# The low half of a weight split by an accumulating SBUF-to-SBUF DMA, in a two-layer float32 encoder

## Chip, cores and metric

One NeuronCore of a Trainium2 chip runs the whole program. The metric is the device time of one execution in microseconds, the median of the runs; smaller is better.

## The reference, cut to what matters

```
for l in range(2):
    hn = rms_norm(h, mix_norm_g[l])
    h = h + (diff_hgrn_mixer(hn, ...) if l == 0 else short_conv_mixer(hn, ...))
    hn = rms_norm(h, mlp_norm_g[l])
    h = h + jnp.square(jax.nn.relu(hn @ mlp_w_up[l])) @ mlp_w_down[l]
return rms_norm(h, final_norm_g)
```

x is 256 x 2048 in float32. Layer 0's mixer has one input projection of 2048 x 8192 (eight heads of differential attention with ALiBi and eight of a two-way gated recurrence) and an output projection of 2048 x 2048. Layer 1's mixer is `(b_gate * conv3(c_gate * h)) @ w_out`, with an input projection of 2048 x 6144 and an output of 2048 x 2048. Each MLP has 2048 x 8192 up and 8192 x 2048 down. All is float32, and the weights, 400 MB in all, are read once.

## The kernel before

**The split of a weight.** TensorE multiplies in float32r. To keep float32's accuracy, every operand is held as a high part (rounded to float32r) and a low part (the rest), and each product is three matmuls: high by high, high by low, low by high. The activations are split once (xT_hi, xT_lo, yT_hi, yT_lo), the weights as they stream in.

**Slots and halves.** The weights come in 400 slots of 1 MB (128 rows x 4 x 512 float32), numbered through the program: 64 for layer 0's input (PROJ_AT), 16 for its output (OUT_AT), 128 for the first MLP (MLP0_AT), 64 for the convolution layer (CONV_AT), 128 for the second MLP (MLP1_AT). `raw` holds RAW = 4 slots. A slot is split in two halves (k = 0 and 1) of 128 x 1024, and w_hi and w_lo are rings of HALVES = 4 halves. So halves 2s and 2s + 1 belong to slot s and half j takes the place of half j - 4.

The engines take a slot in this order:

- SyncE, `load` (L295 to L305): waits until the low parts of slot s - 4 are done, and issues the DMA of slot s into `raw`. From the first MLP on it is one DMA of 1 MB, before that four of 256 KB.
- ScalarE, `split_hi` (L314 to L327): waits for the landing and, for each half, until the half four before has been used by TensorE (`w_used`); then the activation of L326 copies `raw` to w_hi, rounding.
- VectorE, `split_lo` (L329 to L339): waits for `hi_ready`; L337 is w_lo = raw - w_hi, and counts `lo_ready` up by one.
- TensorE, `multiply` (L341 to L359, 12 matmuls of 512 columns a half) or `multiply_T` (L361 to L381, 24 of 256 columns): waits for `lo_ready` of its half and counts `w_used` up at its end.

ScalarE and VectorE stand two slots ahead: while TensorE is at slot s, they split slot s + 2. All queues are in order and written out by hand, one program for each engine; loops (`Fori`) cover the repeated blocks.

**The stages that the change touches.** An MLP (`mlp` in each engine's program) has 16 blocks of 512 hidden columns, each with four up slots (`multiply_T`, result with the hidden units on partitions) and four down slots (`multiply`). In the block's course ScalarE makes the ReLU and the square of the up product (L1072, L1077) and its high part (L1087), VectorE its low part (L1419) and the sums into h (L1195). The convolution layer has 48 input slots in `multiply_T` form and 16 output slots.

**GpSimd (POOL).** Its program is busy in layer 0 (`mix`). After that it only does `rstd_of(n)` for the four later norms (L516, L519, L520), each behind VectorE's sum of squares, and, between norm 2 and norm 3, four products cg = cg * rows2 (L638), each behind VectorE's product of L1459. It issues no DMA.

**The end.** SyncE loads the final norm's gains into raw slot 0 (L474) when slot TOTAL - 4 is split; VectorE scales h by them (L1560), and SyncE stores.

Of the kernel before, what the change touches and what calls it, by code (L numbers as in the profile page):

```python
# [27 lines left out]
F32 = mybir.dt.float32  # L28
F32R = mybir.dt.float32r
U32 = mybir.dt.uint32  # L30
ALU = mybir.AluOpType
ACT = mybir.ActivationFunctionType
AX_X = mybir.AxisListType.X

P = 128
T = 256
# [3 lines left out]
CB = D // 512  # L40
# [5 lines left out]
RAW = 4  # L46
HALVES = 4
# [5 lines left out]
FF_BLOCKS = FF // 512  # L53
MLP_SLOTS = FF_BLOCKS * 8
MLP0_AT = OUT_AT + 16
CONV_AT = MLP0_AT + MLP_SLOTS
CONV_SLOTS = CB * 16
MLP1_AT = CONV_AT + CONV_SLOTS
TOTAL = MLP1_AT + MLP_SLOTS
# [39 lines left out]
def build(nc, x, mix_norm_g, mlp_norm_g, final_norm_g, ab_w_in, ab_w_out, diff_lambda, diff_subln_g,  # L99
          hgrn_lb, hgrn_norm_g, conv_w_in, conv_w, conv_w_out, mlp_w_up, mlp_w_down, out):  # L100
    with ExitStack() as ctx:
        def sb(name, shape, dt=F32):
            return ctx.enter_context(nc.sbuf_tensor(name, shape, dt))
# [4 lines left out]
        def sem(name):  # L108
            return ctx.enter_context(nc.semaphore(name))


        raw = sb("raw", [P, RAW, 4, 512])
        w_hi = sb("w_hi", [P, HALVES, 2, 512], F32R)
        w_lo = sb("w_lo", [P, HALVES, 2, 512], F32R)
# [54 lines left out]
        cg = proj_a[:, :, :, :].rearrange("p a b c -> p (a b c)").rearrange(  # L169
            "p (a b) -> p a b", b=T)  # L170
        cT = lq[:, 1]
        rows2 = bias[:, 0]
# [11 lines left out]

        landed = [sem(f"landed{i}") for i in range(RAW)]
        hi_ready = sem("hi_ready")
        lo_ready = sem("lo_ready")
        w_used = sem("w_used")
        x_in = [sem(f"x_in{i}") for i in range(CB)]
# [6 lines left out]
        pair_read = [sem(f"pair_read{i}") for i in range(2)]  # L196
# [14 lines left out]
        u_ready = sem("u_ready")  # L211
# [38 lines left out]
        def h_read(n):  # L250

            return PAIR_MLP0 + 1 if isinstance(n, int) and n == 0 else n * 3 + (PAIR_MLP0 - 1)
# [29 lines left out]
        def count(scale, const, base, step, i):  # L282

            if isinstance(i, int):
                return scale * (base + step * i) + const
            return i * (scale * step) + (scale * base + const)

        def stand_alone(eng, n):


            if not isinstance(n, int):
                eng.sem_inc(waited, 1)


        def load(sp, base, step, i, src, pieces=1):  # L295

            slot = base % RAW
            if base >= RAW:

                sp.wait_ge(lo_ready, count(2, 2 - 2 * RAW, base, step, i))  # L300
            if pieces == 1:
                sp.dma_start(raw[:, slot], src).then_inc(landed[slot], 16)
                return
            for q in range(pieces):
                sp.dma_start(raw[:, slot, q], src(q)).then_inc(landed[slot], 16)  # L305

        def landed_at(base, step, i):


            each, before = (64, 0) if base < MLP0_AT else (16, 48 * (MLP0_AT // RAW))  # L310
            uses = base // RAW + 1
            return i * (each * step // RAW) + (each * uses + before)

        def split_hi(eng, base, step, i, ks=(0, 1)):  # L314
            if base >= TOTAL:
                return
            slot = base % RAW
            if 0 in ks:

                eng.wait_ge(landed[slot], landed_at(base, step, i))  # L320
            for k in ks:
                ring = (2 * base + k) % HALVES
                if 2 * base + k >= HALVES:

                    eng.wait_ge(w_used, count(2, k + 1 - HALVES, base, step, i))
                nc.scalar.activation(w_hi[:, ring], raw[:, slot, 2 * k:2 * k + 2], ACT.Copy  # L326
                                     ).then_inc(hi_ready, 1)  # L327

        def split_lo(eng, base, step, i, ks=(0, 1)):  # L329
            if base >= TOTAL:  # L330
                return
            slot = base % RAW
            for k in ks:
                ring = (2 * base + k) % HALVES

                eng.wait_ge(hi_ready, count(2, k + 1, base, step, i))
                nc.vector.tensor_tensor(w_lo[:, ring], raw[:, slot, 2 * k:2 * k + 2],  # L337
                                        w_hi[:, ring].bitcast(F32), ALU.subtract
                                        ).then_inc(lo_ready, 1)  # L339

        def multiply(eng, base, step, i, hi, lo, kt0, dst, first, last, ks=(0, 1)):  # L341

            for k in ks:
                ring = (2 * base + k) % HALVES

                eng.wait_ge(lo_ready, count(2, k + 1, base, step, i))
                for q in range(2):
                    kt = kt0 + 2 * k + q
                    begin = first and k == ks[0] and q == 0
                    end = last and k == ks[-1] and q == 1  # L350
                    for tt in range(NT):
                        cols = slice(tt * P, (tt + 1) * P)
                        nc.tensor.matmul(dst[:, tt], hi[:, kt, cols], w_hi[:, ring, q],  # L353
                                         start=begin, stop=False)
                        nc.tensor.matmul(dst[:, tt], hi[:, kt, cols], w_lo[:, ring, q],  # L355
                                         start=False, stop=False)
                        mm = nc.tensor.matmul(dst[:, tt], lo[:, kt, cols], w_hi[:, ring, q],  # L357
                                              start=False, stop=end)
                mm.then_inc(w_used, 1)  # L359

        def multiply_T(eng, base, step, i, kt0, dst, first, last):  # L361

            for k in range(2):
                ring = (2 * base + k) % HALVES

                eng.wait_ge(lo_ready, count(2, k + 1, base, step, i))
                for q in range(2):
                    kt = kt0 + 2 * k + q
                    end = last and k == 1 and q == 1
                    for c in range(4):  # L370
                        cols = slice(c * P, (c + 1) * P)


                        begin = first and k == 0 and q == 0 and c % 2 == 0
                        nc.tensor.matmul(dst[:, c], w_hi[:, ring, q, cols], xT_hi[:, kt],  # L375
                                         start=begin, stop=False)
                        nc.tensor.matmul(dst[:, c], w_hi[:, ring, q, cols], xT_lo[:, kt],  # L377
                                         start=False, stop=False)
                        mm = nc.tensor.matmul(dst[:, c], w_lo[:, ring, q, cols], xT_hi[:, kt],  # L379
                                              start=False, stop=end and c % 2 == 1)  # L380
                mm.then_inc(w_used, 1)  # L381
# [9 lines left out]
        def _(sp):  # L391
# [25 lines left out]
            with sp.Fori(0, HEADS - 1) as i:  # L417
                for p in range(8):
                    load(sp, 8 + p, 8, i,
                         lambda q: head_columns(p // 4, p % 4, bass.ds(i + 1, 1))(q)  # L420
                         .rearrange("p a b n -> p (a b) n"), 4)
# [48 lines left out]
            mlp(MLP1_AT, 1)  # L470


            sp.wait_ge(lo_ready, 2 * (TOTAL - 4) + 2)
            sp.dma_start(raw[:, 0], final_norm_g.rearrange("(a c n) -> a c n", a=1, n=512)  # L474
                         .broadcast_to([P, 4, 512])).then_inc(fin_rows, 16)
            for cb in range(CB):
# [9 lines left out]
        def _(pool):  # L486
# [4 lines left out]
                                    base=0, pattern=[[-1, P]], channel_multiplier=1  # L491
# [21 lines left out]
            def rstd_of(n):  # L513

                pool.wait_ge(sq_sum, n + 1)
                nc.gpsimd.tensor_scalar(meansq[:], meansq[:], 1.0 / D, EPS, ALU.mult, ALU.add  # L516
                                        ).then_inc(rstd_step, 1)
                pool.wait_ge(rstd_step, 2 * n + 1)
                nc.gpsimd.tensor_tensor(rstd[:, n], meansq[:], minus_half[:, 0:NT], ALU.pow)  # L519
                nc.gpsimd.tensor_tensor(rstd2[:, n], meansq[:], minus_one[:], ALU.pow  # L520
                                        ).then_inc(rstd_step, 1)

            rstd_of(0)
            for d in range(2):
                for lv in range(7):
# [5 lines left out]
                                            base=-lo, pattern=[[-2 * m, 64 // m], [0, m]],  # L531
# [4 lines left out]
                                            base=lo + m - 1, pattern=[[2 * m, 64 // m], [0, m]],  # L536
# [91 lines left out]
            with pool.Fori(0, HEADS - 1) as i:  # L628
                mix(i)
            mix(HEADS - 1)  # L630
            for n in range(1, 5):
                rstd_of(n)
                if n == 2:

                    pool.wait_ge(r2_row, 1)
                    for b in range(CB):
                        pool.wait_ge(pair_read[1], h_read(b))
                        nc.gpsimd.tensor_tensor(cg, cg, rows2.unsqueeze(1).broadcast_to([P, 4, T]),  # L638
                                                ALU.mult).then_inc(u_ready, 1)


        def gain_transpose_pe(n, cb):

# [942 lines left out]
```

## Time and profile before

| what | value |
| --- | --- |
| median of 3 runs | 2364.97 us (2364.95 to 2365.18) |
| the profiled execution: its span, first to last instruction | 2362.9 us |
| own time of the profiled execution beside its span | not listed apart; the median stands 2.1 us over the span |
| TensorE matmuls busy | 2332.4 us, 99% |
| VectorE busy | 1462.6 us, 62% |
| ScalarE busy | 1090.2 us, 46% |
| GpSimd busy | 249.8 us, 11% |
| load queue's packets, share of 16 DMA engines | 56.4% |

The span is cut by stage: layer 0's mixer up to about 530 us, the first MLP to about 1240, the convolution layer to about 1610, the second MLP to 2350, and the end. "Busy" is the time in which an engine runs an instruction; waits and the issue of DMAs don't count. Matmuls are pipelined: one of 512 columns shows 389 ns, but the next starts before it ends.

### The profile page before, as it was taken

How to read it: one execution, taken by the hardware profiler on the slowest of the kernel's cores; microseconds unless marked ns; L12 is line 12 of the kernel's file. 1: busy time of each engine (PE TensorE's matmuls, PEld its weight loads, DVE VectorE, ACT ScalarE, POOL GpSimd, SP SyncE). 2: the span in 40 equal slices, each digit the busy share in tenths (PEclk: the TensorE clock that was granted, in tenths of full speed). 3: DMA queues.
4: the chain of work that ended last, by engine and by line, in shares of the span. 5: the costliest groups of instructions: out<-in, count | busy, mean ns of one | idle time of the engine just before them, and what ended most of it. 6: DMA issues, size and time to landing. Idle time of an engine off the chain costs nothing.

```text
span 2362.9 us, 38313 instructions
## 1 busy us (share of the span) xinstructions
PE 2332.4 (99%) x14581; PEld 2108.1 (89%) x14581; DVE 1462.6 (62%) x1686; ACT 1090.2 (46%) x1391; POOL 249.8 (11%) x367
## 2 busy tenths in 40 slices
PE   8999999999999999999999999999999999999997
PEld 6888888789899999999989999998998998998996
DVE  5777777755565565565566564656555556555655
ACT  5555554435444444444445334345444444444443
POOL 4445555500000000000000000000000000000000
PEclk9999999999999999999999999999999999999999
DMA  9555555455555555555555555555555555555553
GB/s 257 162 154 157 145 152 166 145 177 170 189 192 181 192 182 194 180 193 182 190 188 176 187 180 183 192 179 178 194 180 194 181 193 182 191 183 189 189 184 125
DMA packets 316175, 425.78 MB, mean 180 GB/s; under 512 B 10537, under 2 KB 141906, under 8 KB 315986
## 3 DMA queue, kind: packets, MB, share of 16 engines
q1 hardware_dynamic: 316066, 424.92, 56.4%
q8 instruction: 43, 0.70, 0.1%
q14 instruction: 18, 0.15, 0.0%
q10 hardware_dynamic: 48, 0.02, 0.0%
HBM read 422.79 MB, written 2.10 MB: 180 GB/s over the span
## 4 chain that ended last, share of the span: by engine, by line
PE 87%; POOL 6%; issue 4%; ACT 1%; DVE 1%; SPq 1%; DMA 0%; POOLq 0%; DVEq 0%; ACTq 0%
PE pair L353 14%; PE pair L355 14%; PE pair L357 14%; PE m L379 11%; PE m L377 11%; PE m L375 11%; PE pair L379 3%; PE pair L375 3%; PE pair L377 3%; POOL lk L577 1%; PE m L726 1%; POOL even L564 1%; POOL kin L577 1%; PE m L790 1%; POOL lk L589 1%
## 5 line engine op out<-in xcount | busy, mean ns | idle before, releaser
L337 DVE TENSOR_TENSOR w_lo<-raw,w_hi 128x1024 fp32r<-128x1024 f32 x800 | 988.8, 1242 | 855.5 <-ACT w_hi L326 854.5
L326 ACT ACTIVATE w_hi<-raw 128x1024 fp32r<-128x1024 f32 x800 | 846.2, 1059 | 1219.3 <-PE pair L357 633.6
L379 PE MATMUL m<-xT_hi,w_lo 128*128 128x256 f32 x2176 | 615.8, 283 | 0.0
L377 PE MATMUL m<-xT_lo,w_hi 128*128 128x256 f32 x2176 | 615.8, 283 | 0.0
L375 PE MATMUL m<-xT_hi,w_hi 128*128 128x256 f32 x2176 | 615.6, 283 | 0.0
L353 PE MATMUL pair<-w_hi,yT_hi 128*128 128x512 f32 x1280 | 499.8, 391 | 1.0 <-DVE h L1208 0.9
L355 PE MATMUL pair<-w_lo,yT_hi 128*128 128x512 f32 x1280 | 498.4, 389 | 0.0
L357 PE MATMUL pair<-w_hi,yT_lo 128*128 128x512 f32 x1280 | 498.1, 389 | 0.0
L375 PEld LDWEIGHTS m<-xT_hi,w_hi 128*128 128x128 f32 x2176 | 417.7, 192 | 1.2
L377 PEld LDWEIGHTS m<-xT_lo,w_hi 128*128 128x128 f32 x2176 | 417.7, 192 | 1.2
L379 PEld LDWEIGHTS m<-xT_hi,w_lo 128*128 128x128 f32 x2176 | 417.7, 192 | 0.0
L353 PEld LDWEIGHTS pair<-w_hi,yT_hi 128*128 128x128 f32 x1280 | 240.4, 188 | 50.8 <-DVE h L1208 1.4
L357 PEld LDWEIGHTS pair<-w_hi,yT_lo 128*128 128x128 f32 x1280 | 240.3, 188 | 50.3
L355 PEld LDWEIGHTS pair<-w_lo,yT_hi 128*128 128x128 f32 x1280 | 240.5, 188 | 48.1
L1195 DVE SCALAR_TENSOR_TENSOR h<-pair,rstd,h 128x512 f32<-128x512 f32 x288 | 202.0, 743 | 5.8 <-PE pair L357 5.8
L353 PE MATMUL pair<-w_hi,xT_hi 128*128 128x512 f32 x512 | 204.1, 399 | 0.0
L357 PE MATMUL pair<-w_hi,xT_lo 128*128 128x512 f32 x512 | 200.0, 391 | 0.0
L355 PE MATMUL pair<-w_lo,xT_hi 128*128 128x512 f32 x512 | 199.7, 390 | 0.0
L375 PE MATMUL pair<-xT_hi,w_hi 128*128 128x256 f32 x640 | 181.6, 284 | 0.0
L379 PE MATMUL pair<-xT_hi,w_lo 128*128 128x256 f32 x640 | 181.1, 283 | 0.0
L377 PE MATMUL pair<-xT_lo,w_hi 128*128 128x256 f32 x640 | 181.1, 283 | 0.0
L516 POOL TENSOR_SCALAR meansq<-meansq 128x2 f32<-128x2 f32 x5 | 1.0, 193 | 1607.4 <-DVE meansq L1188 1607.4
(147 smaller groups left out, 1711.0 us busy)
## 6 DMA issues: line engine op xcount, KB each, us to landing
raw<-in_mlp_w_up SPq DMA_DIRECT2D x128, 1024.0 KB, 5.2
raw<-in_mlp_w_down SPq DMA_DIRECT2D x128, 1024.0 KB, 5.0
raw<-in_ab_w_in SPq DMA_DIRECT2D x256, 256.0 KB, 3.9
raw<-in_conv_w_in SPq DMA_DIRECT2D x48, 1024.0 KB, 5.2
raw<-in_ab_w_out SPq DMA_DIRECT2D x64, 256.0 KB, 4.1
raw<-in_conv_w_out SPq DMA_DIRECT2D x16, 1024.0 KB, 5.0
h<-in_x SPq DMA_DIRECT2D x4, 512.0 KB, 5.9
out_dram<-h SPq DMA_DIRECT2D x8, 256.0 KB, 2.4
```

The lines of the kernel that those rows point to most:

```text
L326: nc.scalar.activation(w_hi[:, ring], raw[:, slot, 2 * k:2 * k + 2], ACT.Copy).then_inc(hi_ready, 1)
L337: nc.vector.tensor_tensor(w_lo[:, ring], raw[:, slot, 2 * k:2 * k + 2], w_hi[:, ring].bitcast(F32), ALU.subtract).then_inc(lo_ready, 1)
L353: nc.tensor.matmul(dst[:, tt], hi[:, kt, cols], w_hi[:, ring, q], start=begin, stop=False)
L355: nc.tensor.matmul(dst[:, tt], hi[:, kt, cols], w_lo[:, ring, q], start=False, stop=False)
L357: mm = nc.tensor.matmul(dst[:, tt], lo[:, kt, cols], w_hi[:, ring, q], start=False, stop=end)
L375: nc.tensor.matmul(dst[:, c], w_hi[:, ring, q, cols], xT_hi[:, kt], start=begin, stop=False)
L377: nc.tensor.matmul(dst[:, c], w_hi[:, ring, q, cols], xT_lo[:, kt], start=False, stop=False)
L379: mm = nc.tensor.matmul(dst[:, c], w_lo[:, ring, q, cols], xT_hi[:, kt], start=False, stop=end and c % 2 == 1)
L564: nc.gpsimd.tensor_tensor(both(even, lv)[:, :, :, 1], first[:, :, 0::2], second[:, :, 0::2], ALU.mult)
L577: mark(nc.gpsimd.tensor_tensor(dst.rearrange("p (a b) -> p a b", b=m), src.rearrange("p (a b) -> p a b", b=m), factor.unsqueeze(2).broadca ...
L589: mark(nc.gpsimd.tensor_copy(dst.rearrange("p (a b c) -> p a b c", b=2, c=m)[:, :, 1], kin[:, 1].rearrange("p (a b c) -> p a b c", b=2, c= ...
L1195: ins = nc.vector.scalar_tensor_tensor(out=h[:, tt, cols], in0=pair[cb % 2][:, tt], scalar=factor[:, tt:tt + 1], in1=h[:, tt, cols], op0=A ...
```

## The change

From slot MLP0_AT on, the second half (k = 1) of each of the 320 slots gets its low part in another way. ScalarE writes, behind the high part of that half, w_lo = -raw, rounded to float32r as the high part is (an activation with a scale of -1.0, counted by `neg_ready`). GpSimd waits for it and issues a DMA within SBUF that adds raw to w_lo, 128 rows x 1024 float32, 512 KB (`add_lo`, `accum_op=ALU.add`, counted by `lo_added`, one semaphore for each raw slot, 16 for each DMA). The sum is raw minus its rounded value, the same low part. VectorE's subtraction for that half goes; the first halves (k = 0) and all of layer 0's mixer stay as they are.

TensorE waits for `lo_added` in front of second halves (`wait_lo`), and SyncE's `load` for both `lo_added` and `lo_ready` of the slot that it overwrites. GpSimd's program gets the 320 DMAs in slot order, with `rstd_of` and the four products of the convolution layer placed between them (`mlp_los`, `scale_u`).

```diff
             slot = base % RAW
+            if base >= MLP0_AT + RAW:
+                sp.wait_ge(lo_added[slot], lo_added_at(base - RAW, step, i))
+                stand_alone(sp, i if step else 0)
             if base >= RAW:
-                sp.wait_ge(lo_ready, count(2, 2 - 2 * RAW, base, step, i))
+                sp.wait_ge(lo_ready, lo_at(base - RAW, step, i, 1))
...
+        def wait_lo(eng, base, step, i, k):
+            if base >= MLP0_AT and k == 1:
+                eng.wait_ge(lo_added[base % RAW], lo_added_at(base, step, i))
+            else:
+                eng.wait_ge(lo_ready, lo_at(base, step, i, k))
...
                 nc.scalar.activation(w_hi[:, ring], raw[:, slot, 2 * k:2 * k + 2], ACT.Copy
                                      ).then_inc(hi_ready, 1)
+                if base >= MLP0_AT and k == 1:
+                    nc.scalar.activation(w_lo[:, ring], raw[:, slot, 2:4], ACT.Copy, scale=-1.0
+                                         ).then_inc(neg_ready, 1)
+
+        def add_lo(pool, base, step, i):
+            slot, ring = base % RAW, (2 * base + 1) % HALVES
+            pool.wait_ge(neg_ready, count(1, 1 - MLP0_AT, base, step, i))
+            stand_alone(pool, i if step else 0)
+            pool.dma_start(w_lo[:, ring].bitcast(F32), raw[:, slot, 2:4], accum_op=ALU.add
+                           ).then_inc(lo_added[slot], 16)
...
             for k in ks:
+                if base >= MLP0_AT and k == 1:
+                    continue
...
-                eng.wait_ge(lo_ready, count(2, k + 1, base, step, i))
+                wait_lo(eng, base, step, i, k)
...
-            sp.wait_ge(lo_ready, 2 * (TOTAL - 4) + 2)
+            sp.wait_ge(lo_ready, lo_at(TOTAL - 4, 0, 0, 0))
+            sp.wait_ge(lo_added[0], lo_added_at(TOTAL - 4, 0, 0))
...
+            def mlp_los(at, n):
+                for p in range(4):
+                    add_lo(pool, at + p, 0, 0)
                 rstd_of(n)
+                for p in range(4):
+                    add_lo(pool, at + 4 + p, 0, 0)
+                with pool.Fori(0, FF_BLOCKS - 1) as i:
+                    for p in range(8):
+                        add_lo(pool, at + 8 + p, 8, i)
...
+            mlp_los(MLP0_AT, 1)
+            for p in range(12):
+                if p == 4:
+                    rstd_of(2)
+                if p == 10:
                     pool.wait_ge(r2_row, 1)
+                    scale_u(0)
+                add_lo(pool, CONV_AT + p, 0, 0)
+            with pool.Fori(0, CB - 2) as i:
+                for p in range(16):
+                    if p == 10:
+                        scale_u(i + 1)
+                    add_lo(pool, CONV_AT + 12 + p, 16, i)
...
+            mlp_los(MLP1_AT, 3)
+            rstd_of(4)
```

## Rows read from the trace of the kernel before

**Rows 1.** The page: busy time of each engine over the span
```profile
span 2362.9 us, 38313 instructions
PE 2332.4 (99%) x14581; PEld 2108.1 (89%) x14581; DVE 1462.6 (62%) x1686; ACT 1090.2 (46%) x1391; POOL 249.8 (11%) x367
```

**Rows 2.** Busy time in stretches: one up, one down product, the changed stages, the end
```profile
core 0: us, PE busy (x) PEld busy (x) DVE busy (x) ACT busy (x) POOL busy (x), PEclk, DMA share, GB/s
702.50:725.50 23.00, 23.00 (x194) 23.00 (x193) 12.32 (x12) 9.51 (x10) 0.00 (x0) 1.00 0.57 184
725.50:747.30 21.80, 21.80 (x99) 18.04 (x98) 13.76 (x14) 10.39 (x12) 0.00 (x0) 1.00 0.59 189
537.00:2350.00 1813.00, 1813.00 (x12018) 1676.08 (x12016) 1065.63 (x1100) 815.38 (x944) 14.26 (x13) 1.00 0.56 184
2350.00:2362.90 12.90, 0.06 (x1) 0.00 (x0) 6.96 (x11) 1.45 (x4) 1.55 (x3) 0.70 0.45 163
```

**Rows 3.** ScalarE's timeline in one MLP block: start, length, what, idle before
```profile
705.42 1.06 ACT L326 ACTIVATE w_hi<-raw 128x1024 fp32r<-128x1024 f32 x1 [1.81 <-PE m L379]
708.30 1.06 ACT L326 ACTIVATE w_hi<-raw 128x1024 fp32r<-128x1024 f32 x1 [1.82 <-PE m L379]
...
725.58 1.06 ACT L326 ACTIVATE w_hi<-raw 128x1024 fp32r<-128x1024 f32 x1 [1.82 <-PE m L379]
726.55 1.06 ACT L1072 ACTIVATE sm<-m 128x512 f32<-128x512 f32 x2
727.50 1.15 ACT L1077 ACTIVATE sm<-sm 128x512 f32<-128x512 f32 x2
728.54 1.06 ACT L326 ACTIVATE w_hi<-raw 128x1024 fp32r<-128x1024 f32 x1
731.04 1.06 ACT L326 ACTIVATE w_hi<-raw 128x1024 fp32r<-128x1024 f32 x1 [1.45 <-PE pair L357]
733.76 1.06 ACT L326 ACTIVATE w_hi<-raw 128x1024 fp32r<-128x1024 f32 x1 [1.66 <-PE pair L357]
736.48 1.06 ACT L326 ACTIVATE w_hi<-raw 128x1024 fp32r<-128x1024 f32 x1 [1.66 <-PE pair L357]
```

**Rows 4.** Groups of instructions, one MLP block (702.5 to 747.3)
```profile
L337 DVE TENSOR_TENSOR w_lo<-raw,w_hi 128x1024 fp32r<-128x1024 f32 x16 | 19.6, 1225 | 18.7 <-ACT w_hi L326 18.7
L326 ACT ACTIVATE w_hi<-raw 128x1024 fp32r<-128x1024 f32 x16 | 17.0, 1060 | 24.9 <-PE m L379 13.5 <-PE pair L357 11.4
```

**Rows 5.** One load: issue; DMA in 40 slices from 738.9 to 744.9; one full us
```profile
738.97 0.37 SPq L302 DMA_DIRECT2D raw<-in_mlp_w_up  x1
...
DMA  0000000377799989888999999999973000000000
q1 hardware_dynamic: 528, 1.05, 53.0%
raw<-in_mlp_w_up SPq DMA_DIRECT2D x1, 1024.0 KB, 5.1
...
742.00:743.00 1.00, 1.00 (x6) 0.84 (x5) 0.00 (x0) 0.98 (x1) 0.00 (x0) 1.00 1.04 406
```

**Rows 6.** GpSimd's timeline from 530 on: start, length, what, idle before
```profile
564.79 0.19 POOL L516 TENSOR_SCALAR meansq<-meansq 128x2 f32<-128x2 f32 x1 [79.94 <-DVE meansq L1188]
565.07 0.70 POOL L519 TENSOR_TENSOR rstd<-meansq,minus_half 128x2 f32<-128x2 f32 x1
565.74 0.70 POOL L520 TENSOR_TENSOR rstd<-meansq,minus_one 128x2 f32<-128x2 f32 x1
...
1315.56 2.40 POOL L638 TENSOR_TENSOR proj_a<-proj_a,bias 128x1024 f32<-128x1024 f32 x1 [28.49 <-DVE proj_a L1459]
```

**Rows 7.** Waits of SyncE's queue: what for, us in total, times, longest
```profile
SPq L302 <- DVE w_lo L337: 1612.6, 320, 7.9
```

**Rows 8.** ScalarE's timeline at the first MLP's norm
```profile
562.32 1.06 ACT L326 ACTIVATE w_hi<-raw 128x1024 fp32r<-128x1024 f32 x1 [0.28 <-PE pair L379]
```

**Rows 9.** The final norm's load, and VectorE's use of it
```profile
2325.24 0.34 SPq L474 DMA_DIRECT2D raw<-in_final_norm_g  x1
...
2354.37 5.39 DVE L1560 SCALAR_TENSOR_TENSOR h<-h,rstd,raw 128x512 f32<-128x512 f32 x8 [1.76 <-POOL rstd L520]
```

More of the change, by code:

```diff
@@ L186, in build @@
         hi_ready = sem("hi_ready")
+        neg_ready = sem("neg_ready")
+        lo_added = [sem(f"lo_added{i}") for i in range(RAW)]
         lo_ready = sem("lo_ready")
@@ L305, in load, with lo_at, lo_added_at @@
                 sp.dma_start(raw[:, slot, q], src(q)).then_inc(landed[slot], 16)
+        def lo_at(base, step, i, k):
+            if base < MLP0_AT:
+                return count(2, k + 1, base, step, i)
+            return count(1, MLP0_AT + 1, base, step, i)
+        def lo_added_at(base, step, i):
+            return i * (16 * step // RAW) + 16 * ((base - MLP0_AT) // RAW + 1)
+        def wait_lo(eng, base, step, i, k):
[3 more added lines that the diff above has]
+                eng.wait_ge(lo_ready, lo_at(base, step, i, k))
         def landed_at(base, step, i):
@@ L364, in multiply_T @@
                 ring = (2 * base + k) % HALVES
-                eng.wait_ge(lo_ready, count(2, k + 1, base, step, i))
+                wait_lo(eng, base, step, i, k)
                 for q in range(2):
@@ L630, in _, with scale_u @@
             mix(HEADS - 1)
-            for n in range(1, 5):
+            def mlp_los(at, n):
+                for p in range(4):
+                    add_lo(pool, at + p, 0, 0)
                 rstd_of(n)
-                if n == 2:
-                    pool.wait_ge(r2_row, 1)
[L636 to L639, printed above, removed]
+                for p in range(4):
[3 more added lines that the diff above has]
+                        add_lo(pool, at + 8 + p, 8, i)
+            def scale_u(b):
+                pool.wait_ge(pair_read[1], h_read(b))
+                stand_alone(pool, b)
+                nc.gpsimd.tensor_tensor(cg, cg, rows2.unsqueeze(1).broadcast_to([P, 4, T]),
+                                        ALU.mult).then_inc(u_ready, 1)
+            mlp_los(MLP0_AT, 1)
[3 more added lines that the diff above has]
+                if p == 10:
+                    pool.wait_ge(r2_row, 1)
+                    scale_u(0)
[5 more added lines that the diff above has]
+                    add_lo(pool, CONV_AT + 12 + p, 16, i)
+            for p in range(20):
+                if p == 10:
+                    scale_u(CB - 1)
+                add_lo(pool, CONV_AT + CONV_SLOTS - 20 + p, 0, 0)
+            mlp_los(MLP1_AT, 3)
+            rstd_of(4)
         def gain_transpose_pe(n, cb):
```

## The prediction

> **What bounds the kernel now.** I read the page's busy times first, then stretches, then who waits for whom. TensorE (PE) is busy 99% of the span, VectorE (DVE) 62% and ScalarE (ACT) 46% [rows 1]. In the stages that the change touches the share is whole: PE is busy 1813.00 of the 1813.00 us from 537 to 2350, at a granted clock of 1.00 (full, 2.4 GHz), while DVE stands idle 41% of that stretch; the 12.9 us behind it are the final norm and the stores [rows 2]. So the pace there is PE's own. From one release of a ring half to the next (two starts of ACT's high split, each set off by PE) it is 708.30 - 705.42 = 2.88 us in an up product and 736.48 - 733.76 = 2.72 us in a down product [rows 3]: a slot of two halves takes 5.76 or 5.44 us. Of the 320 slots from the first MLP on, 176 are of the first kind (64 in each MLP, 48 in the convolution layer) and 144 of the second, 5.62 us in the mean. No PE time is left to gain; the question is only whether the new path of the low part stays within its cover.
>
> The span is 2362.9 us and the median of the runs 2364.97, so some 2.1 us lie around the span; the sums below are differences and go on the median.
>
> **What it removes.** 320 of the 800 DVE subtractions, at 1225 ns each in the steady stage [rows 4]: 392 us of DVE work. None of it ends a wait of PE, so it is worth nothing: the cover is PE itself.
>
> **What it adds on ACT.** 320 negated copies of 128x1024, at the 1060 ns of the high split of the same shape [rows 4]: 339 us. ACT has 1.82 us between two splits of an up product and 1.66 in a down product, so the copy fits. At one place of each MLP block it doesn't quite. Behind the copy that follows the split of 725.58, the two ReLUs and two squares, 2.0 us, end at about 729.7, and the next high split starts 1.2 us late; the high splits from 731.04 on are on time again [rows 3]. A half has three halves of time (8.16 or 8.64 us) from its release to its use, against the 1.06 + 1.23 us that the two splits take, so a late high split costs nothing.
>
> **What it adds behind ACT.** One half in two now runs: release, high split, negated copy, GpSimd (POOL) issues the DMA, it lands, PE. Split and copy end 2.2 us after the release (2 x 1.06 and a hop). What is left until PE stands waiting is 8.16 - 2.2 = 5.96 us in a down product and 6.44 in an up product. The DMA must issue and land in that. The trace has no DMA from POOL and no accumulation, so its three parts are bounded from rows.
>
> *Issue.* SyncE's load is issued at 738.97 and its first packets run about 1.0 us later, in the eighth of the 0.15 us slices [rows 5]. POOL's own instructions take from 0.19 to 2.40 us [rows 6]. I take 1.5 us to the first packet, between 1.0 and 2.4, the POOL side having to write out the descriptors of 128 rows itself.
>
> *Data, X.* A 1 MB load keeps the 16 engines busy for 53.0% of 6.0 us, 3.2 us, and runs at about 406 GB/s at its best, in the one us in which all are busy [rows 5]. The accumulation reads 512 KB of raw weights and 512 KB of w_lo and writes 512 KB. If only what is written counts, X = 524 KB / 406 = 1.3 us; if what is read counts, 1.05 MB / 406 = 2.6 us, or 3.2 at the load's mean pace; if three passes run one after another, 3.9. The nearest row is the load, which puts the same 1 MB through the read side, so I take between 2.6 and 3.2: X = 2.8, the ends being 1.3 and 3.9.
>
> The Trainium skill speaks to this choice in "Collectives: The Full Stack", section "The bandwidth ceiling: the fold count and why AG ≠ RS ≠ AR": an add in the DMA engine costs no cycles of its own but needs two source reads on one ring, which halves the rate. By that X is twice a copy's, which is the value by reads; no row here shows an accumulation.
>
> *Landing.* Packets end near 743.5, and the load lands 5.1 us after issue, at 744.1: 0.6 us. So the DMA alone takes A = 1.5 + 2.8 + 0.6 = 4.9 us, inside both covers, with 1.1 us to spare in a down product.
>
> *Contention.* It isn't alone. SyncE's load into a raw slot now also waits for that slot's accumulation (before, for the second subtraction [rows 7]), so its packets start 1.0 + 0.1 us after an accumulation lands, at A + 1.1 us from that one's issue, while the next accumulation is issued one slot (P) after this one, so that its packets start P + 1.5 us after this one's issue. With A near P these two meet. If both share the engines evenly, the accumulation runs alone for d = (A + 1.1) - (P + 1.5) = A - P - 0.4 us and at half speed after that: A = 1.5 + d + 2(X - d) + 0.6, which with X = 2.8 is 2A = 8.1 + P. PE closes the circle over two slots: its half (2.8), split and copy and hop (2.2), and A: 2P = 5.0 + A. Together 1.5 P = 9.05, P = 6.03 and A = 7.1 us, against 5.62 now: +0.41 us a slot, 320 times, 131 us. PE's new waits are then at the second half of each slot, on the accumulation.
>
> By the same two lines X = 2.6 gives P = 5.90 (+90 us), 3.2 gives 6.30 (+218 us), 3.9 gives 6.77 (+368 us), and the change costs nothing below X = 2.2, where P meets 5.62. Engine work bounds it less: 3.2 + 2.8 = 6.0 us a slot by the load's mean pace, but 2.6 + 2.6 = 5.2 at 406 GB/s.
>
> **What else moves.** The raw ring: a load now goes out about 2.2 + 7.1 = 9.3 us after the release that starts its slot's second high split, and ACT wants the data three slots and a half after it, at 3 x 5.6 + 2.7 = 19.5; with 5.1 to 8 us to land, 2 to 5 us remain, nothing. DVE's rstd factors: POOL takes the add of the fifth slot of a normed stage behind the 1.65 us of the three POOL instructions of the norm. ACT's second high split of that slot starts at 562.32, its copy would end at about 564.5, and POOL's norm ends at 566.44 [rows 6, 8]. That is 2 us later once in each of three norms: at most 6 us, and it goes into a stream that waits already; I count 3. POOL's four products of the convolution layer (2.40 us [rows 6]) start when a slot's seventh neighbour is done, 4 us ahead of the next due copy, so no accumulation waits for them. The final norm's load has 29 us in hand (issued 2325.24, used 2354.37) [rows 9]. Sum: 2365 + 131 + 3 = 2499, say 2500 us.
>
> **Rivals.** (a) *Hidden: no change.* X at 2.2 or less, so that A stays under 5.96 us even beside the load, DVE's subtractions go, ACT and the queues take the work, PE doesn't notice: 2363 to 2368 us. For it: the engines rest some 42% of the time [rows 2], and a load's packets at full activity pass 406 GB/s, so a stream that is paid by bytes written needs only 1.3 us. Against it: the accumulation has two sources. The Trainium skill's page "DMA: Bandwidth & Descriptors", section "Anatomy of one DMA — SWDGE (gpsimd) path", gives a DMA issued from POOL about 2.0 us plus its bytes at 436 GB/s, by which this one would land in 3.2 us and be hidden; no row here has such a DMA. This is the case on the other side, and it decides at A = 5.96 us. 0.2.
>
> (b) *The DMA engines become the bound.* Accumulation costs more than its reads (X of 3.9 or more), 3.2 + 3.9 = 7.1 us of engine work in a slot of 5.62. P = 6.8 to 7.1, 2365 + 320 x 1.2 to 1.5 = 2750 to 2840 us. For it: nothing excludes that adding in 32 bits is slower than moving. 0.17.
>
> (c) *A gain.* It would need PE waits that DVE causes now; between 537 and 2350 there are none [rows 2]. Outside, the added work doesn't act. 0.03, at about 2358 us.
>
> My case (accumulation late by a little in every slot, paid by its reads, 2400 to 2740 us): 0.6.
>
> **Numbers.** A measurement of this kernel can tell about 0.2%, 4.7 us, from no change. Faster 0.03 (c); same 0.2 (a); slower 0.77 (0.6 + 0.17). The predicted time is that of my case, 2500 us. The range must take in (a), as leaving it out would leave out 2 in 10 by itself, so it begins at 2362; at the top it ends at 2740, where X is 3.9 with a loaded queue, and leaves out (b). The likeliest case's own range is 2400 to 2740.
>
> **What would show it.** Right: PE idle in front of the second half's first product, released by the accumulating DMA, some 0.4 us a slot, and nearly none in front of first halves; the second queue beside the load queue at about half of a slot's engine time (2.8 x 320 us is 36% of a 2500 us span); issue to landing of 6.5 to 7.5 us; DVE near 1070 us busy and ACT near 1430. Rival (a): landing under 5.96 us and PE still without waits. Rival (b): all 16 engines busy over 90% of each slot and loads landing late too, with ACT waiting for raw. My price fails if accumulation has a pace that no row here has, or if POOL needs more than 2.4 us to issue one; then POOL would show the time between its DMAs.

## The result and the profile after

The changed kernel takes 2699.12 us (median of 4 runs, 2693.69 to 2713.24) against 2364.98 before: a ratio of 1.142, with a 95% interval of 1.139 to 1.145. It is slower by 334 us. The profiled executions differ by nearly the same, 2691.6 against 2362.9 us in span.

The page of the changed kernel; these lines answer to [rows 1], and behind them stand two groups of instructions, the two DMA queues, two lines of the DMA issues (KB, median us to landing) and the landings of the 320 additions:

```profile
span 2691.6 us, 39327 instructions
PE 2431.9 (90%) x14581; PEld 2159.1 (80%) x14581; DVE 1084.8 (40%) x1366; ACT 1388.5 (52%) x1711; POOL 525.3 (20%) x687
...
L357 POOL DMA_DIRECT2D w_lo<-raw x320 | 275.5, 861 | 1879.6 <-ACT w_lo L349 1829.8
L349 ACT ACTIVATE w_lo<-raw 128x1024 fp32r<-128x1024 f32 x320 | 333.4, 1042 | 0.0
...
q1 hardware_dynamic: 316066, 424.92, 48.2%
q0 software_dynamic: 46080, 167.79, 33.7%
...
w_lo<-raw POOLq DMA_DIRECT2D x320, 512.0 KB, 5.7
raw<-in_mlp_w_up SPq DMA_DIRECT2D x128, 1024.0 KB, 6.1
...
DMA to landing us min/median/max: 4.5/5.7/9.5
```

TensorE was idle for 30.5 us of its span before and is for 259.7 now: 229 us more. Its busy time has grown by 99.5 us over the same 14581 matmuls. The two make up the 329 us. The additions take 33.7% of 2691.6 us on 16 engines, which is 2.83 us for each of the 320. The idle time has one releaser. TensorE's waits (engine, line, what for; us in total, times, longest):

```profile
PE pair L386 <- DMA w_lo<-raw: 119.4, 61, 3.7
PE m L408 <- DMA w_lo<-raw: 89.9, 50, 3.4
PE pair L408 <- DMA w_lo<-raw: 19.5, 13, 3.0
```

That is 228.8 us in 124 waits, so 124 of the 320 slots wait, for 1.8 us in the mean; the other 196 don't show one. The busy time that was added is mostly the clock. The changed stages (as [rows 2], third line), and the core's mean clock:

```profile
537.00:2680.00 2143.00, 1912.45 (x12020) 1727.03 (x12018) 688.74 (x783) 1113.81 (x1265) 289.75 (x333) 0.97 0.88 234
...
core 0: 2691.6 us, clock 0.971
```

A mean of 0.971 between the two levels of 1.2 and 2.4 GHz says that 5.8% of the span, 156 us, ran at the lower one, where it was 0.998 and some 10 us before. 146 us more at half speed cost at most 73 us of TensorE's work. The rest of the 99.5, 27 us or more, is put down to waits too short to be listed, which lengthen the first matmul of a half; no run shows it by itself, but e_order below has 26 us of it at an unchanged clock.

One late addition, in full. GpSimd's, ScalarE's and SyncE's timelines from 899 to 907 (start, length):

```profile
900.95 0.86 POOL L357 DMA_DIRECT2D w_lo<-raw  x1 [4.89 <-ACT w_lo L349]
906.71 0.86 POOL L357 DMA_DIRECT2D w_lo<-raw  x1 [4.90 <-ACT w_lo L349]
...
904.13 1.06 ACT L346 ACTIVATE w_hi<-raw 128x1024 fp32r<-128x1024 f32 x1 [1.77 <-PE m L412]
905.09 1.04 ACT L349 ACTIVATE w_lo<-raw 128x1024 fp32r<-128x1024 f32 x1
...
901.13 0.37 SPq L306 DMA_DIRECT2D raw<-in_mlp_w_down  x1
```

The chain of work, and TensorE's next instructions:

```profile
900.95 9.38 DMA w_lo<-raw
...
910.36 0.58 PE L408 MATMUL m<-xT_hi,w_hi 128*128 128x256 f32 x1 [3.40 <-DMA w_lo<-raw]
910.74 0.41 PE L410 MATMUL m<-xT_lo,w_hi 128*128 128x256 f32 x1
```

And four of the microseconds between (columns: PE, PEld, DVE, ACT, POOL busy, PE clock, DMA share, GB/s):

```profile
902.00:903.00 1.00, 1.00 (x11) 1.00 (x10) 0.61 (x1) 0.36 (x1) 0.00 (x0) 1.00 0.95 63
904.00:905.00 1.00, 1.00 (x10) 1.00 (x10) 0.82 (x2) 0.87 (x1) 0.00 (x0) 1.00 1.05 344
907.00:908.00 1.00, 0.00 (x0) 0.00 (x0) 0.00 (x0) 1.00 (x1) 0.57 (x1) 1.00 1.04 238
909.00:910.00 1.00, 0.00 (x0) 0.00 (x0) 0.32 (x1) 0.00 (x0) 0.00 (x0) 0.50 1.09 217
```

The addition is issued at 900.95 and lands at 910.33, after 9.4 us, where most take 4.5 to 6 us. SyncE's load went out 0.18 us after it. TensorE stands idle for 3.40 us, the granted clock falls to 0.50 meanwhile, and its first two matmuls of 256 columns take 0.58 and 0.41 us where 0.28 is the rule. How the two DMAs share the engines, counted from the packet records (packets that start in each 0.25 us, of all 16 engines; the load has 512, the addition 128; eight of the slices, not in a row):

```
us       load  addition
902.15     14      0
903.15      5      0
904.15     45      0
904.90     34      0
905.40     34      1      first packet of the addition, 4.7 us after its issue
906.40     19     11
907.65     11     14
908.40     14     11
```

So the addition isn't served at all until 324 of the load's packets have ended (338 have started), well over half; from then on the two go packet by packet, about one to one.

The same holds over all 320 additions of the changed kernel, sorted by when the load nearest to them in time was issued. In 66 cases that was between 1.0 us before the addition and 0.3 us after it: their first packets come after 3.2 to 5.3 us, and TensorE waits for every one of them, 151 us in all. In 213 cases no load was issued from 2 us before to 0.5 us after: first packets after 1.4 to 2.5 us, 24 waits, 30 us in all. The other 41 lie between. What holds the addition back inside the queues, no record shows.

For this kernel and the runs below, the same records over all 320 additions (us from issue, to the start of the first and the end of the last packet, the latter some 0.3 before the landing):

```
run             first: median  95%   last: median  95%
changed kernel          1.77  4.80           5.40  8.42
e_bg                    1.71  3.59           7.27  8.71
e_copy                  1.49  4.40           3.93  6.59
e_half                  1.92  4.89           4.45  7.07
e_order                 1.58  1.98           5.12  6.01
e_anti                  2.21  4.93           6.09  8.53
```

The cover can be read too: ScalarE's high split starts on TensorE's release at 904.13, and the issue is at 906.71. So 2.58 us are gone before the addition is out, and 8.16 - 2.58 = 5.58 us remain in a down product, 8.64 - 2.58 = 6.06 in an up product.

### The profile page after: what moved, and what is told of

It is laid out like the page before. It is cut to its first block, busy times and chain, and to the rows that moved or that the text cites. A ratio compares the mean times of both kernels' runs of the same rounds, so it can differ in the third digit from the quotient of the medians.

```text
span 2691.6 us, 39327 instructions
## 1 busy us (share of the span) xinstructions
PE 2431.9 (90%) x14581; PEld 2159.1 (80%) x14581; DVE 1084.8 (40%) x1366; ACT 1388.5 (52%) x1711; POOL 525.3 (20%) x687
## 3 DMA queue, kind: packets, MB, share of 16 engines
q0 software_dynamic: 46080, 167.79, 33.7%
## 4 chain that ended last, share of the span: by engine, by line
PE 40%; DMA 35%; issue 10%; ACT 8%; POOL 5%; DVE 1%; SPq 0%; POOLq 0%; ACTq 0%; DVEq 0%
DMA w_lo<-raw 35%; PE pair L386 7%; PE pair L390 6%; PE pair L388 6%; PE m L408 5%; ACT w_lo L349 5%; PE m L412 5%; PE m L410 5%; ACT w_hi L346 2%; PE pair L408 1%; POOL lk L611 1%; PE m L786 1%; PE pair L412 1%; PE pair L410 1%; POOL even L598 1%
## 5 line engine op out<-in xcount | busy, mean ns | idle before, releaser
L370 DVE TENSOR_TENSOR w_lo<-raw,w_hi 128x1024 fp32r<-128x1024 f32 x480 | 596.9, 1252 | 1319.5 <-ACT w_hi L346 1319.1
L408 PE MATMUL m<-xT_hi,w_hi 128*128 128x256 f32 x2176 | 635.3, 292 | 90.2 <-DMA w_lo<-raw 89.9
L357 POOL DMA_DIRECT2D w_lo<-raw x320 | 275.5, 861 | 1879.6 <-ACT w_lo L349 1829.8
L386 PE MATMUL pair<-w_hi,yT_hi 128*128 128x512 f32 x1280 | 521.1, 407 | 120.5 <-DMA w_lo<-raw 119.4
L408 PEld LDWEIGHTS m<-xT_hi,w_hi 128*128 128x128 f32 x2176 | 431.0, 198 | 102.8 <-DMA w_lo<-raw 101.4
L388 PE MATMUL pair<-w_lo,yT_hi 128*128 128x512 f32 x1280 | 511.6, 400 | 0.0
L390 PE MATMUL pair<-w_hi,yT_lo 128*128 128x512 f32 x1280 | 511.2, 399 | 0.0
L410 PEld LDWEIGHTS m<-xT_lo,w_hi 128*128 128x128 f32 x2176 | 430.9, 198 | 1.3
L412 PEld LDWEIGHTS m<-xT_hi,w_lo 128*128 128x128 f32 x2176 | 430.2, 198 | 0.0
L349 ACT ACTIVATE w_lo<-raw 128x1024 fp32r<-128x1024 f32 x320 | 333.4, 1042 | 0.0
```

What stands on the lines that cost most here:

```text
L349: nc.scalar.activation(w_lo[:, ring], raw[:, slot, 2:4], ACT.Copy, scale=-1.0).then_inc(neg_ready, 1)
L357: pool.dma_start(w_lo[:, ring].bitcast(F32), raw[:, slot, 2:4], accum_op=ALU.add).then_inc(lo_added[slot], 16)
```

## The experiments

The theory was that the 320 additions cost time only where one lands after its cover, that this comes from a start behind a load, and that waits are then paid twice, by the clock. The rivals were ScalarE's copies, the engine work of the DMAs, a fixed cost of GpSimd's DMAs, and an even sharing in which order doesn't matter.

**e_act: ScalarE's part alone.** On the kernel before:

```diff
+                if base >= MLP0_AT and k == 1:
+                    nc.scalar.activation(w_lo[:, ring], raw[:, slot, 2:4], ACT.Copy, scale=-1.0
+                                         ).then_inc(neg_ready, 1)
```

> The kernel before, with ScalarE's 320 negated copies added in front of VectorE's subtraction of the same halves; no DMA within SBUF. Theory (the additions land late for TensorE, and the clock falls behind the waits): the copy is covered, 2365 to 2368 us, TensorE without waits between 537 and 2350. Rival (ScalarE's extra 339 us make the halves late): 2450 us or more, TensorE waiting for w_lo.

Measured: 2366.0 us, ratio 1.0004 (0.9994 to 1.0013). TensorE is busy all of the time from 537 to 2350. The copies cost nothing.

```profile
537.00:2350.00 1813.00, 1813.00 (x12019) 1676.18 (x12018) 1044.18 (x1101) 1114.14 (x1265) 20.58 (x13) 1.00 0.56 184
```

**e_bg: all of the work, none of TensorE's waits.** The kernel before with the copies and additions going into spare buffers; VectorE still makes every low part:

```diff
+                    nc.scalar.activation(w_add[slot].bitcast(F32R), raw[:, slot, 2:4], ACT.Copy, scale=-1.0
+                                         ).then_inc(neg_ready, 1)
...
+            pool.dma_start(w_add[slot], raw[:, slot, 2:4], accum_op=ALU.add
+                           ).then_inc(lo_added[slot], 16)
```

> The kernel before, with all of the new work beside it: negated copies and additions go into a scratch buffer, and only SyncE's loads wait for them; TensorE goes on waiting for VectorE's subtraction alone. Theory (what costs is that TensorE waits for an addition that started behind a load): 2365 to 2380 us, with the additions' landings as uneven as in the changed kernel. Rival (the 16 DMA engines cannot carry 3.2 + 2.8 us a slot): the loads fall behind, ScalarE waits for raw, 2500 us or more.

Measured: 2367.77 us, ratio 1.0011 (1.0001 to 1.0021). Its queues, its stretch, and two waits of ScalarE, in an execution of 2373.86 us, 6 us over the median:

```profile
q1 hardware_dynamic: 316066, 424.92, 53.5%
q0 software_dynamic: 46080, 167.79, 37.9%
...
537.00:2350.00 1813.00, 1808.64 (x11987) 1669.45 (x11986) 1056.78 (x1096) 1104.60 (x1251) 290.94 (x332) 1.00 1.02 276
...
ACT w_hi L346 <- DMA raw<-in_mlp_w_up: 113.0, 55, 4.5
ACT w_hi L346 <- DMA raw<-in_mlp_w_down: 84.1, 40, 5.6
```

The 16 engines show a share of 1.02 (packets overlap) and move 276 GB/s, against 184 before [rows 2], and the pace of 5.62 us a slot holds. The additions land later here than in the changed kernel (their last packets end after 7.3 us in the median against 5.4), as loads and additions follow each other faster, and it costs 3 us in all. So the engines can carry the work; a late landing costs only who waits for it. ScalarE begins to wait for the MLPs' loads, 197 us here where neither the kernel before nor the changed one has such a wait, and TensorE hardly feels it (busy 1808.64 of 1813 us): the engines are near their end.

**e_lead: the same additions one slot earlier.** ScalarE negates the second half of slot s + 1 behind the high split of slot s, into a ring of four (two of w_lo, two unused parts of yT_hi); TensorE and SyncE also wait for the high half, as the addition no longer tells that it is done:

```diff
-                if base >= MLP0_AT and k == 1:
-                    nc.scalar.activation(w_lo[:, ring], raw[:, slot, 2:4], ACT.Copy, scale=-1.0
-                                         ).then_inc(neg_ready, 1)
+                if k == 1 and MLP0_AT <= base <= MLP0_AT + 1:
+                    negate(eng, base, step, i)
+                if k == 1 and MLP0_AT + 2 <= base + 1 < TOTAL:
+                    negate(eng, base + 1, step, i)
```

> The changed kernel with the negated copy and the accumulation one slot earlier, into a ring of four buffers; DMA, copies and loads are as many and as large. The cover grows from 5.5 to 11 us. Theory (the accumulation's lateness alone costs): landings of 6.5 to 8 us as in the run with scratch buffers, TensorE without waits from 537 on, 2366 to 2380 us. Rival (the accumulation's engine work, 3.2 + 2.8 us a slot, sets the pace once TensorE has to have its result): 2450 us or more.

Measured: 2367.25 us, ratio 1.0011 (1.0002 to 1.0021). Its issues, its stretch and TensorE's only waits for an addition:

```profile
w_lo<-raw POOLq DMA_DIRECT2D x160, 512.0 KB, 7.8
yT_hi<-raw POOLq DMA_DIRECT2D x160, 512.0 KB, 7.8
...
537.00:2350.00 1813.00, 1811.93 (x12011) 1674.89 (x12010) 681.25 (x781) 1113.45 (x1261) 290.15 (x333) 1.00 1.01 277
...
PE pair L426 <- DMA w_lo<-raw: 0.6, 2, 0.4
PE m L426 <- DMA w_lo<-raw: 0.4, 1, 0.4
```

Here TensorE takes its low parts from the additions, they land 2 us later than in the changed kernel, and of the 334 us some 3 are left. This settles that the loss is lateness, not work.

**e_copy and e_half: how much the data time does.** In e_copy a plain copy takes the place of the addition, so that w_lo becomes raw and the subtraction is left out of those halves; in e_half the addition has half the columns and VectorE does the others.

```diff
-            pool.dma_start(w_lo[:, ring].bitcast(F32), raw[:, slot, 2:4], accum_op=ALU.add
+            pool.dma_start(w_lo[:, ring].bitcast(F32), raw[:, slot, 2:4]
```

```diff
-            pool.dma_start(w_lo[:, ring].bitcast(F32), raw[:, slot, 2:4], accum_op=ALU.add
+            pool.dma_start(w_lo[:, ring, 1].bitcast(F32), raw[:, slot, 3], accum_op=ALU.add
```

> The changed kernel with plain copies in place of the additions (w_lo becomes raw itself, the addition is left out). If an addition is paid by what it reads: packets of 164 to 168 ns in place of 327, landing 1.3 us earlier in the median (4.4 us in place of 5.7), and by the theory the waits of TensorE fall from 229 us to 40 to 90, the time to 2410 to 2480 us. If an addition costs no more than a copy, packets stay near 327 ns and the time near 2700 us.

> The changed kernel with additions of half the size: 128x512, 256 KB; VectorE subtracts the other 128x512 of each second half. Theory: data time 1.4 us in place of 2.8, but the start behind a load stays up to 4.8 us late; landing of 4.3 us in the median with a tail to 8 us, 2400 to 2470 us. Rival (a fixed cost for each DMA from GpSimd is what costs): 2600 us or more.

Measured: 2466.81 us (1.0435, 1.0418 to 1.0452) and 2473.95 us (1.0449, 1.0421 to 1.0477), the second 4 us above its forecast, with a landing of 4.8 us where 4.3 was expected. The packet records give 159 ns in the median for a copied packet of 4 KB, 328 for an added one. Each run's second queue, e_copy first:

```profile
q0 software_dynamic: 46080, 167.79, 18.0%
w_lo<-raw POOLq DMA_DIRECT2D x320, 512.0 KB, 4.4
```

```profile
q0 software_dynamic: 46080, 83.91, 19.9%
w_lo<-raw POOLq DMA_DIRECT2D x320, 256.0 KB, 4.8
```

An added byte costs two copied ones. e_copy differs in one more thing: its first packets come 0.3 us sooner at best (1.09 us after the issue against 1.42). TensorE waits 69 us in e_copy and 83 us in e_half, in waits of up to 2.5 us; the clock, 0.996 in both, stays up. With data time nearly halved the late start remains (4.4 and 4.9 us at the 95% mark of the table), and so do 102 and 109 us.

**e_order and e_anti: who goes first.** SyncE's load into a freed slot waits, in e_order, for the next addition to have been issued, and in e_anti for the next negated copy, just before it:

```diff
                 sp.wait_ge(lo_added[slot], lo_added_at(base - RAW, step, i))
                 stand_alone(sp, i if step else 0)
+                sp.wait_ge(add_out, count(1, 1 - MLP0_AT, base - 3, step, i))
+                stand_alone(sp, i if step else 0)
...
+            nc.gpsimd.memset(tick[:], 0.0).then_inc(add_out, 1)
```

```diff
+                sp.wait_ge(neg_ready, count(1, 1 - MLP0_AT, base - 3, step, i))
+                stand_alone(sp, i if step else 0)
```

> The changed kernel; SyncE issues the load into a freed slot only when GpSimd has issued the next accumulation (a tiny memset behind each accumulation tells it), so no accumulation stands right behind a load of the same moment. Theory (a load issued up to a microsecond ahead keeps an accumulation from starting, 1.4 us becoming up to 4.8): first packets 1.4 to 1.8 us after issue nearly always, landing of 5 to 6 us with a short tail, waits of TensorE 40 to 120 us in place of 229, 2400 to 2500 us. Rival (the two share the engines evenly in any order): no better than 2650 us.

> The changed kernel; SyncE holds each load back until ScalarE has finished the next negated copy, so that load and accumulation go out together and the load's packets are first in every slot. Theory: nearly every accumulation starts 3 to 5 us after its issue and lands after 7 to 9 us, TensorE waits in most slots, its clock is at 1.2 GHz more often, 2780 to 2950 us. Rival (order doesn't matter): within 1% of the changed kernel's 2699 us.

Measured: 2415.49 us for e_order (1.0218, 1.0201 to 1.0235), 2985.54 us for e_anti (1.2601, 1.2557 to 1.2646). Same DMAs, same bytes, 570 us apart. TensorE's waits, e_order first:

```profile
PE pair L394 <- DMA w_lo<-raw: 11.1, 15, 3.2
PE m L416 <- DMA w_lo<-raw: 10.2, 18, 1.3
PE pair L416 <- DMA w_lo<-raw: 1.8, 3, 1.3
```

```profile
PE pair L388 <- DMA w_lo<-raw: 196.7, 71, 3.1
PE m L410 <- DMA w_lo<-raw: 179.7, 68, 5.3
PE pair L410 <- DMA w_lo<-raw: 45.4, 20, 3.9
```

e_order has first packets after 1.4 to 2.0 us in all but a few slots and landings of 5.4 us in the median, right at its cover. The listed waits are 23 us, below the forecast of 40 to 120, and it still keeps 51 us. How, TensorE's busy time and ScalarE's releases show (the first line is from the page):

```profile
PE 2358.4 (98%) x14581; PEld 2102.8 (87%) x14581; DVE 1083.5 (45%) x1366; ACT 1388.0 (58%) x1711; POOL 559.7 (23%) x1007
...
917.69 1.06 ACT L350 ACTIVATE w_hi<-raw 128x1024 fp32r<-128x1024 f32 x1 [0.50 <-PE pair L398]
920.41 1.06 ACT L350 ACTIVATE w_hi<-raw 128x1024 fp32r<-128x1024 f32 x1 [0.71 <-PE pair L398]
923.33 1.06 ACT L350 ACTIVATE w_hi<-raw 128x1024 fp32r<-128x1024 f32 x1 [1.85 <-PE pair L398]
```

One half takes 2.72 us, the next 2.92: a wait of 0.2 us. Most such waits no list shows; they stand in the busy time, 26 us more than before at a mean clock of 0.997 against 0.998.

e_anti passed its forecast by 35 us, and in another way: not every addition is late, but every second one (158 of the 320 have their first packet after more than 3 us). In GpSimd's issues at 905.73, 916.04, 921.42 and 930.12 the first packets come after 1.92, 4.72, 1.93 and 4.84 us. A late addition stops TensorE, the next copy comes early against the load, and the turn after that meets the load again. In 157 slots the nearest load was issued between 1.0 us before the addition and 0.3 us after it, and these have 157 of the 159 waits; of the others nearly all have theirs 2 to 6 us later. A rival is that e_anti's loads come late because they are held back: but ScalarE shows no wait for a load in these stages. Its mean clock is 0.936, so 382 us at 1.2 GHz.

**e_order_half: both remedies.** e_order with e_half's additions.

> Both remedies that keep the ring as it is: additions of half the size (128x512, VectorE does the rest) and loads held back until the next addition is issued. Theory (landing against a cover of 5.5 us is all that counts, and start order and data time add up in it): landing near 4.0 to 4.6 us with no tail over 5.5, no waits of TensorE on it, 2365 to 2372 us. Rival (the order's run keeps its 50 us through something else, GpSimd's or SyncE's extra instructions): 2390 us or more, as these are here too.

Measured: 2365.8 us, ratio 1.0005 (0.9996 to 1.0015); TensorE waits for no addition, and they land after 3.6 us in the median, sooner than forecast:

```profile
w_lo<-raw POOLq DMA_DIRECT2D x320, 256.0 KB, 3.6
```

GpSimd's and SyncE's extra instructions of e_order are here too, so they weren't its 51 us.

## Why the prediction was right and wrong

The sign and the place held, and so did the mechanism in the large: TensorE waits for late additions. The loss was put at 135 us and is 334. That 2699 us lies inside the range is luck: the top of 2740 us stood for a data time X of 3.9 us, and X measured 2.83, for which the prediction's own sum gives some 2500.

**What held.** No gain from the 392 us of subtractions, which are gone from VectorE (busy 1084.8 us where it was 1462.6) without any effect; ScalarE's copies free (e_act; 333.4 us, 339 forecast); waits at second halves only, on the addition; 1.5 us to the first packet (1.42 when alone); A = 4.9 us alone, roughly (the shortest landing is 4.5); and the data term, X = 2.8 us against 2.83 measured. The rule of the Trainium skill that agrees with that choice ("Collectives: The Full Stack", section "The bandwidth ceiling: the fold count and why AG ≠ RS ≠ AR": two source reads on one ring) is borne out by e_copy: 328 against 159 ns a packet. Rival (a) lost. The estimate of 3.2 us to landing, worked out from the Trainium skill's "DMA: Bandwidth & Descriptors", section "Anatomy of one DMA — SWDGE (gpsimd) path", doesn't hold for this addition, of which the shortest took 4.5 us. It is nearer to a copy: in e_copy the shortest of the 320 landed after 2.8 us, with 4.4 in the median beside the loads. Rival (b) lost by e_bg and e_lead.

**The step that failed is "Contention".** It let the two DMAs share evenly from the first packet on, and closed the circle with one mean: A = 7.1, P = 6.03, 0.41 us lost in each slot. Both halves were wrong. The mean landing is 6.1 us, below 7.1, and by 2P = 5.0 + A such a mean would have cost nothing. But the landings spread from 4.5 to 9.5 us, since an addition issued with a load is first held back and only then shares. TensorE, with no slack of its own, loses each excess and gets nothing back for the early ones: 229 us of listed waits, in 124 slots of 1.8 us each, where the step had 131 us in 320. With the clock and the short waits a slot takes 6.70 us in the mean (2143 us for 320). A pace taken from a mean is right only where every slot waits.

**A term that was missing: the clock.** The prediction had waits of 0.4 us in each slot and none of 3.4 us in some. With waits of that length TensorE's granted clock fell to 0.50, and the 146 us more at that level account for up to 73 us of the 99.5 us of added busy time. The split is worked out from rows, not tried: no run kept the waits and held the clock.

**A small one: the hop.** The cover was put at 5.96 us with 0.1 us from ScalarE to GpSimd. From the end of the copy (906.13) to the issue (906.71) it takes 0.58 us, so the cover is 5.58; over all 320 the median of that hop is 0.57. What it costs is an estimate: over e_order's landings the excess above 5.58 us sums to 52 us, and above 5.96 to 27.

The terms for the norms (3 us) and the raw ring (0) weren't tested apart; e_lead, which has both, ends at 3 us. Two forecasts of busy time were a little off: ScalarE's 1430 us is 1388.5, as its instructions overlap in the profile (the copy of 905.09 starts before the split of 904.13 ends), and VectorE's 1070 is 1084.8. And by [rows 2] the engines rested 44% of the time, not 42.

## What to carry to other kernels

Where one engine is busy all the time, moving others' work to a DMA can't gain, and it costs by the tail of the landing times, not by their mean: read the longest landing, with the other queue's load beside it, against the cover. If it doesn't fit, start it a stage earlier (e_lead: some 331 of the 334 us came back) or put it ahead of the competing transfer (e_order: some 283). Before costing two queues by shared bandwidth, ask which of them has its packets in first, and spread them over the issue times that occur.

## What the runs showed of the hardware that was not expected

- Here two queues shared the DMA engines about one packet to one only after the load had a head start: an addition issued 0.18 us before a 1 MB load had its first packet 4.7 us after issue, not 1.4, with 324 of the load's 512 packets through. All 66 additions of the changed kernel with a load issued from 1.0 us before to 0.3 us after them started 3.2 to 5.3 us after issue.
- The engines carried 276 GB/s of loads and additions at a share of 1.02, against 184 at 0.56 before, with TensorE busy 1808.64 of 1813 us (e_bg).
- The order of two DMAs alone moved the kernel between 2415 and 2985 us, and in the slower one (e_anti) the late additions fell into a pattern of every second slot.
